# A two-layer hybrid transformer pair: the long convolutions' transforms as three products of high and low parts

## The reference

```python
def hyena_filter(n, w1, b1, freq, w2, b2, w3):
    ...                                  # a small MLP of the positions, two-sided, normalised to sum 1
    return two_sided / jnp.sum(jnp.abs(two_sided), axis=0, keepdims=True)
# per channel: g = cv * x1 (both short convolutions of projections of the normed input)
#              y = longconv(g, filter) + bias * g ; then y * x0, gated
```

## Time and profile before

| | |
|---|---|
| median of the runs | 1718.23 us (1717.48 to 1720.56) |
| the profiled execution | 1713.17 us |
| its span, first to last instruction | 1711.4 us |
| mean granted clock of TensorE | 0.98 |
| TensorE busy | 1606.1 us, 94% |
| VectorE, ScalarE, GpSimd busy | 63%, 49%, 9% |

### The profile page before, as it was taken

One profiled execution on the slowest core, in us unless ns is written; L12 is line 12 of the kernel. 1 busy time (PEld: TensorE's weight loads), 2 busy tenths in 40 slices (PEclk: granted clock), 3 DMA queues, 4 the chain that ended last, 5 costly groups with the idle time before them and its releaser, 6 DMA issues.

```text
span 1711.4 us, 23418 instructions
## 1 busy us (share of the span) xinstructions
PE 1606.1 (94%) x9108; PEld 1347.5 (79%) x9108; DVE 1077.7 (63%) x1999; ACT 830.6 (49%) x1511; POOL 147.2 (9%) x145
## 2 busy tenths in 40 slices
PE   7988999988889999989999998999997979999998
PEld 7967999877778888867778876887786868887886
DVE  7777777776667868754564657325546565464565
ACT  5855555555556555532203456533335255445564
POOL 0110111110000213100000010000001000000000
PEclk9989999999999999989999999999999989999999
DMA  7526655553265545434302111224422314242333
GB/s 251 168 88 212 225 189 186 173 197 101 98 193 173 181 134 173 144 109 165 136 1 74 50 50 37 87 86 172 136 74 87 111 49 131 79 136 76 122 111 123
DMA packets 61886, 217.69 MB, mean 127 GB/s; under 512 B 7888, under 2 KB 8144, under 8 KB 61648
## 3 DMA queue, kind: packets, MB, share of 16 engines
q1 hardware_dynamic: 58608, 212.40, 37.0%
q10 hardware_dynamic: 3168, 3.80, 0.7%
HBM read 215.09 MB, written 1.05 MB: 126 GB/s over the span
## 4 chain that ended last, share of the span: by engine, by line
PE 66%; DVE 12%; ACT 11%; issue 8%; POOL 2%; ACTq 1%; DMA 0%; DVEq 0%; POOLq 0%
PE PS L328 18%; PE PS L330 17%; PE PS L329 17%; DVE WL L304 3%; ACT WH L293 3%; PE PS L2642 2%; PE PS L2010 2%; PE PS L2019 2%; POOL AR L1532 2%; PE PS L779 1%; PE PS L2084 1%; PE PS L485 1%; PE PS L2061 1%; ACT TMP L396 1%; PE PS L2673 1%
## 5 line engine op out<-in xcount | busy, mean ns | idle before, releaser
L304 DVE TENSOR_TENSOR WL<-RAWB,WH 128x1024 fp32r<-128x1024 f32 x346 | 427.1, 1239 | 255.8 <-ACT WH L293 249.7
L328 PE MATMUL PS<-RH,WH 128*128 128x256 f32 (+1 forms) x1560 | 505.6, 324 | 19.7 <-DVE RH L509 4.0
L329 PE MATMUL PS<-RH,WH 128*128 128x256 f32 (+1 forms) x1560 | 492.6, 316 | 0.0
L330 PE MATMUL PS<-RH,WL 128*128 128x256 f32 (+1 forms) x1560 | 492.3, 316 | 0.0
L293 ACT CAST WH<-RAWB 128x1024 fp32r<-128x1024 f32 x346 | 358.5, 1041 | 247.6 <-PE PS L330 192.8
L328 PEld LDWEIGHTS PS<-RH,WH 128*128 128x128 f32 x1560 | 300.6, 193 | 55.1 <-issue 11.2
L328 PE MATMUL PS<-WH,RH 128*128 128x512 f32 (+1 forms) x768 | 307.2, 400 | 16.0 <-DVE WL L304 8.6
L329 PEld LDWEIGHTS PS<-RH,WH 128*128 128x128 f32 x1560 | 300.7, 193 | 18.2 <-issue 0.2
L330 PEld LDWEIGHTS PS<-RH,WL 128*128 128x128 f32 x1560 | 300.0, 192 | 18.5
L329 PE MATMUL PS<-WL,RH 128*128 128x512 f32 (+1 forms) x768 | 298.8, 389 | 0.0
L330 PE MATMUL PS<-WH,RH 128*128 128x512 f32 (+1 forms) x768 | 298.4, 389 | 0.0
(11 more groups left out here) (353 smaller groups left out, 1642.3 us busy)
## 6 DMA issues: line engine op xcount, KB each, us to landing
RAWB<-ws SPq DMA_DIRECT2D x394, 512.0 KB, 3.5
TMP<-gains ACTq DMA_DIRECT2D x8, 256.0 KB, 2.9
CS<-cs SPq DMA_DIRECT2D x1, 1472.0 KB, 9.1
X<-x SPq DMA_DIRECT2D x2, 512.0 KB, 4.0
X<-ctx SPq DMA_DIRECT2D x2, 512.0 KB, 8.1
AR<-dec ACTq DMA_DIRECT2D x2, 512.0 KB, 7.0
out<-X SPq DMA_DIRECT2D x4, 256.0 KB, 2.0
AR<-rgw SPq DMA_DIRECT2D x1, 512.0 KB, 5.1
```

The source lines that it names most:

```text
L304: dve.e.tensor_tensor(k.WL[:, i % SPL, :], k.RAWB[:, i % RAW, :], k.WH[:, i % SPL, :].bitcast(F32), ALU.subtract).then_inc(*dve.done("wl", i))
L328: pe.e.matmul(o, wh, xh, start=first, stop=False)
L329: pe.e.matmul(o, wh, xl, start=False, stop=False)
L330: return pe.e.matmul(o, wl, xh, start=False, stop=last)
```

## The change

The inputs and tables of both transforms become f32r pairs, high and low part, and each f32 matmul becomes three f32r ones (`three`): forward 24, inverse 48 in a unit.

- The forward table's pair lies in the WH/WL place of chunk last + 1 (`last` is the chunk of the last cv projection), written by ScalarE and VectorE at j = 7. The inverse table's pair lies in RH, written at j = 5.
- A turned input's pair lies in the places of chunks last and last - 1: ScalarE writes the high part from PSUM, VectorE the low part and frees the bank.
- Of the complex product's four results (SPC, C1) ScalarE writes the high part, GpSimd the low part, into a ring of six pairs in RH (unit 3's second half into the place of chunk last).
- The bias comes by a DMA on ScalarE's queue at j = 1 (a fifth row of `gains`), and GpSimd adds it to HF's real rows. L2321 goes; ScalarE copies the inverse's result from PSUM into G.
- The chunks last + 1 and last + 2 are split only when the places are free: ScalarE casts them after unit 3's high parts, VectorE after unit 3's product.

```diff
-        self.GT = k.ring("e2gt", [view(8192 + 1024 * i, 2, 512) for i in range(2)])
+        self.SPP = k.ring("e2spp", [(k.RH[:, a:a + 512], k.RH[:, a + 512:a + 1024]) for a in range(10240, 16384, 1024)])
+        self.last = k.ws.chunk("even2", "cv", 7)
+        self.HYB = view(9216, 1024)
...
-        self.dft = lambda n, f: k.C("dft")[:, 512 * n + 128 * f:512 * n + 128 * f + 128]
-        self.idft = lambda f: k.C("idft")[:, 256 * f:256 * f + 256]
+        self.idft = k.RH[:, 8192:9216], k.RH[:, 9216:10240]
+    def place(self, k, n):
+        return k.WH[:, n % SPL, :], k.WL[:, n % SPL, :]
+    def turned(self, k, u):
+        return [t.rearrange("p (a b) -> p a b", a=2) for t in self.place(k, self.last - u % 2)]
+    def forwards(self, k, n, f):
+        return [t[:, 512 * n + 128 * f:512 * n + 128 * f + 128] for t in self.place(k, self.last + 1)]
+    def back(self, f):
+        return [t[:, 256 * f:256 * f + 256] for t in self.idft]
+    def product(self, u, fb, part):
+        return self.C1 if (fb, part) == (1, 1) else self.SPC
+    def parts(self, k, u, fb, part):
+        if u == 3 and fb:
+            return [t[:, 512 * part:512 * part + 512] for t in self.place(k, self.last)]
+        return self.SPP.of(u, fb, part)
...
-SPEC_STEPS = [(*SPEC_UNITS[u], p) for u, p in rounds([3] * 4)]
+SPEC_PARTS = [(0, 0), (0, 1), (1, 0), (1, 1)]
+SPEC_STEPS = rounds([3] * 4)
...
@@ even2_pe
-    for q, c, p in SPEC_STEPS:
+    for u, p in SPEC_STEPS:
+        q, c = SPEC_UNITS[u]
         if p == 0:
             for tb in range(2):
                 b = k.ps.take(pe, s, "gt", q, c, tb)
                     t = pe.e.transpose(b[:, 128 * jj:128 * jj + 128], L.G[:, 4 * c + jj, c0:c0 + 128], k.ident)
                 t.then_inc(*pe.done(s, "gt", q, c, tb))
         elif p == 1:
+            pe.wait_ge(*k.DVE.at(s, "table", 0))
             for tb in range(2):
-                pe.wait_ge(*k.ACT.at(s, "gt", q, c, tb))
-            g = L.GT.of(s, q, c)
+                pe.wait_ge(*k.DVE.at(s, "gt", q, c, tb))
+            gh, gl = L.turned(k, u)
             for fb in range(2):
                 for part in range(2):
-                    b = k.ps.take(pe, s, "u", q, c, fb, part)
+                    b = k.ps.take(pe, s, "u", u, fb, part)
                     for n in range(2):
-                        mm = pe.e.matmul(b, L.dft(n, 2 * part + fb), g[:, n, :], start=n == 0, stop=n == 1)
-                    mm.then_inc(*pe.done(s, "u", q, c, fb, part))
-            L.GT.free(pe, s, q, c)
+                        mm = three(pe, b, L.forwards(k, n, 2 * part + fb), (gh[:, n, :], gl[:, n, :]), n == 0, n == 1)
+                    mm.then_inc(*pe.done(s, "u", u, fb, part))
         else:
-            rows = [L.SPC.of(s, q, c, 0, 0), L.SPC.of(s, q, c, 1, 0), L.SPC.of(s, q, c, 0, 1), L.C1.of(s, q, c, 1, 1)]
-            pe.wait_ge(*k.DVE.at(s, "spec", q, c))
+            pe.wait_ge(*k.DVE.at(s, "table", 1))
+            for fb, part in SPEC_PARTS:
+                pe.wait_ge(*k.POOL.at(s, "low", u, fb, part))
+            rows = [L.parts(k, u, f % 2, f // 2) for f in range(4)]
             for jj in range(4):
                 b = k.ps.take(pe, s, "y", q, 4 * c + jj)
+                cols = slice(128 * jj, 128 * jj + 128)
                 for f in range(4):
-                    mm = pe.e.matmul(b[:, 0:256], rows[f][:, 128 * jj:128 * jj + 128], L.idft(f), start=f == 0, stop=f == 3)
+                    mm = three(pe, b[:, 0:256], [t[:, cols] for t in rows[f]], L.back(f), f == 0, f == 3)
                 mm.then_inc(*pe.done(s, "y", q, 4 * c + jj))
-            for name in ((0, 0), (1, 0), (0, 1)):
-                L.SPC.free(pe, s, q, c, *name)
-            L.C1.free(pe, s, q, c, 1, 1)
+            for fb, part in SPEC_PARTS:
+                L.SPP.free(pe, u, fb, part)
...
@@ even2_act
     for j in range(8):
-        cast_to(k, act, k.ws.chunk(s, "x1", j) + 2)
+        cast_to(k, act, min(k.ws.chunk(s, "x1", j) + 2, L.last))
         x = k.sq.take(act, s, "x1", j)
         conv3_act(k, act, s, "x1", j, x, k.P("ecw", 24 + 8 + j), k.P("ecb", 8 + j))
-        cast_to(k, act, k.ws.chunk(s, "cv", j) + 2)
+        cast_to(k, act, min(k.ws.chunk(s, "cv", j) + 2, L.last))
         conv3_act(k, act, s, "cv", j, L.G[:, j, :], k.P("ecw", 24 + 16 + j), k.P("ecb", 16 + j))
-    for q, c, p in SPEC_STEPS:
+        if j == 1:
+            act.wait_ge(*k.DVE.at(s, "hf", 1, 3))
+            act.wait_ge(*k.PE.at(s, "hf", 1, 3))
+            act.e.dma_start(L.HYB, k.gains[4]).then_inc(k.s_hyb, 16)
+        if j == 5:
+            act.wait_ge(k.s_cs2, 16)
+            act_(L.idft[0], k.C("idft"), ACT.Copy).then_inc(*act.done(s, "table", 1))
+        if j == 7:
+            act.wait_ge(*k.PE.at("weights", before(k, L.last + 1)))
+            act_(L.place(k, L.last + 1)[0], k.C("dft"), ACT.Copy).then_inc(*act.done(s, "table", 0))
+    for u, p in SPEC_STEPS:
+        q, c = SPEC_UNITS[u]
         if p == 0:
-            g = L.GT.take(act, s, q, c)
+            act.wait_ge(*k.PE.at("weights", L.last - u % 2))
+            act.wait_ge(*k.PE.at(s, "u", u - 2, 1, 1))
             for tb in range(2):
                 act.wait_ge(*k.PE.at(s, "gt", q, c, tb))
-                act_(g[:, tb, :], k.ps.of(s, "gt", q, c, tb), ACT.Copy).then_inc(*act.done(s, "gt", q, c, tb))
-                k.ps.free(act, s, "gt", q, c, tb)
+                act_(L.turned(k, u)[0][:, tb, :], k.ps.of(s, "gt", q, c, tb), ACT.Copy).then_inc(
+                    *act.done(s, "gt", q, c, tb))
+        elif p == 1:
+            for fb, part in SPEC_PARTS:
+                if u == 3 and fb:
+                    act.wait_ge(*k.PE.at(s, "u", 2, 1, 1))
+                else:
+                    L.SPP.take(act, u, fb, part)
+                act.wait_ge(*k.DVE.at(s, "spec", u, fb, part))
+                act_(L.parts(k, u, fb, part)[0], L.product(u, fb, part).of(u, fb, part), ACT.Copy).then_inc(
+                    *act.done(s, "high", u, fb, part))
+            if u == 3:
+                act.wait_ge(*k.PE.at(s, "u", 3, 1, 1))
+                cast_to(k, act, L.last + 2)
+        else:
+            for j in range(4 * c, 4 * c + 4):
+                act.wait_ge(*k.PE.at(s, "y", q, j))
+                act_(L.G[:, j, 256 * q:256 * q + 256], k.ps.of(s, "y", q, j)[:, 0:256], ACT.Copy).then_inc(
+                    *act.done(s, "conv", j))
+                k.ps.free(act, s, "y", q, j)
...
@@ even2_dve
     for j in range(8):
-        rest_to(k, dve, k.ws.chunk(s, "x1", j) + 2)
+        rest_to(k, dve, min(k.ws.chunk(s, "x1", j) + 2, L.last))
...
-        rest_to(k, dve, k.ws.chunk(s, "cv", j) + 2)
+        rest_to(k, dve, min(k.ws.chunk(s, "cv", j) + 2, L.last))
         conv3_dve(k, dve, s, "cv", j, L.G[:, j, :], k.P("ecw", 16 + j), k.P("ecw", 48 + 16 + j))
...
-    for q, c, p in SPEC_STEPS:
-        if p == 1:
+        if j == 5:
+            dve.wait_ge(*k.ACT.at(s, "table", 1))
+            v.tensor_tensor(L.idft[1], k.C("idft"), L.idft[0].bitcast(F32), ALU.subtract).then_inc(*dve.done(s, "table", 1))
+        if j == 7:
+            hi, lo = L.place(k, L.last + 1)
+            dve.wait_ge(*k.ACT.at(s, "table", 0))
+            v.tensor_tensor(lo, k.C("dft"), hi.bitcast(F32), ALU.subtract).then_inc(*dve.done(s, "table", 0))
+    for u, p in SPEC_STEPS:
+        q, c = SPEC_UNITS[u]
+        if p == 0:
+            gh, gl = L.turned(k, u)
+            for tb in range(2):
+                dve.wait_ge(*k.ACT.at(s, "gt", q, c, tb))
+                v.tensor_tensor(gl[:, tb, :], k.ps.of(s, "gt", q, c, tb), gh[:, tb, :].bitcast(F32), ALU.subtract).then_inc(
+                    *dve.done(s, "gt", q, c, tb))
+                k.ps.free(dve, s, "gt", q, c, tb)
+        elif p == 1:
             cc = slice(512 * c, 512 * c + 512)
+            dve.wait_ge(*k.POOL.at(s, "biased"))
             for fb in range(2):
...
-                v.tensor_tensor(a, a, y, ALU.subtract).then_inc(*dve.done())
+                v.tensor_tensor(a, a, y, ALU.subtract).then_inc(*dve.done(s, "spec", u, fb, 0))
...
-                v.tensor_tensor(x, x, y, ALU.add).then_inc(*dve.done(s, "spec", q, c))
-        elif p == 2:
-            for j in range(4 * c, 4 * c + 4):
-                g = L.G[:, j, 256 * q:256 * q + 256]
-                dve.wait_ge(*k.PE.at(s, "y", q, j))
-                v.scalar_tensor_tensor(g, g, k.P("hyb", j), k.ps.of(s, "y", q, j)[:, 0:256], ALU.mult,
-                                       ALU.add).then_inc(*dve.done(s, "conv", j))
-                k.ps.free(dve, s, "y", q, j)
+                v.tensor_tensor(x, x, y, ALU.add).then_inc(*dve.done(s, "spec", u, fb, 1))
+    rest_to(k, dve, L.last + 2)
...
@@ even2_dve, stage x0
+        dve.wait_ge(*k.ACT.at(s, "conv", j))
...
@@ even2_pool
     L, s = Even2(k), "even2"
+    pool.wait_ge(k.s_hyb, 16)
+    for f in range(2):
+        hr = L.HF[:, f, :]
+        pool.wait_ge(*k.DVE.at(s, "hf", 1, f))
```

(54 more changed lines are left out.)

## The result

Over 20 runs each the changed kernel took 1722.03 us in the median and the one before 1714.76; the ratio is 1.0039, with a 95% interval of 1.0028 to 1.0050: 6.7 us slower by the ratio (4.8 to 8.6), 7.3 by the two medians. The profiled execution of the changed kernel has a span of 1715.0 us in 1716.77. That is only 3.6 us more than the profiled execution before: it reached the stretch of the change 1.1 us earlier and took 2.6 us less behind it, in stages that the edit hardly touches.

What follows compares the result with a forecast made beforehand. TensorE bounded the stretch before; the chain was expected to move to VectorE: 4.0 us less, then 7.3 for the port and 3.2 for the clock, 6.5 us more, 1724.7 us on the median; range 1715 to 1730.

Steps and rivals of the forecast that it cites:

- TensorE's own work: Four forward and four inverse units: three products of parts replace each f32 product, 10.3 us less if TensorE stayed busy.
- The opening: Start of the stretch: the table's and first unit's low parts on VectorE delay TensorE's first forward by 3.6 us.
- The hand-offs between units: VectorE waits for ScalarE and low parts: 2.65 us between units 0 and 1, 4.15 between 1 and 2.
- The port: VectorE operations reading two SBUF tensors wait while GpSimd subtracts: 13 times 0.56 us, 7.3 us on the chain.
- meetings: Spectrum operations with two SBUF inputs arriving while GpSimd works: three per unit, one between units 2 and 3, 13 in all.
- The tail: After the last spectrum: one high part, one GpSimd low part and three hand-offs, 2.3 us, before the last inverse.
- The clock: TensorE's granted clock falls after idle times at the opening and ahead of the last inverse: 1.6 us each, 3.2.
- A third fall: An idle time of 2 to 3 us ahead of the first inverse slows only what has slack; nothing counted.
- Rival 1: GpSimd's and VectorE's operations don't meet: 4.0 us less, 1.5 back for the clock, 1715.7 us; chance 0.15.
- Rival 2: GpSimd and VectorE meet but the clock stays at 1.00: 3.3 us more, 1721.5 us; chance 0.15.
- Rival 3: TensorE stays the bound in the stretch: 10.3 us less, 1707.9 us; chance 0.05 together with another rival.

Runs made afterwards that it cites:

- e7: The inverse half of the change alone, forwards in f32 as in the kernel before: stretch 57.47 us, ratio to before 0.9987.
- e6: The forward half of the change alone, inverse in f32 as in the kernel before, nothing on GpSimd: stretch 58.47 us, ratio to before 0.9988.
- e5: Changed kernel with spectrum products in place in PSUM, forward table split earlier, units 0 and 1 turned ahead of the last projection: stretch 52.27 us, ratio to before 0.9965.
- e1: Changed kernel with the spectrum's products left in place in PSUM, so no operation reads two SBUF tensors: stretch 56.98 us, ratio to before 0.9981.
- e2: Changed kernel with each GpSimd subtraction covering 8 of 512 columns: stretch 56.48 us, ratio to before 0.9979.
- e4: Changed kernel with useless TensorE products ahead of the first forward (15) and the last inverse (18): stretch 62.03 us, ratio to before 1.0020.
- e8: The inverse half of the change alone, with the spectrum's products in place in PSUM: stretch 54.98 us, ratio to before 0.9957.

## Why the prediction was right

The forecast was 6.5 us more on the kernel; 6.7 was measured, and 7.3 in the stretch. The forecast of 1724.7 us stood on a median of three runs, 1718.23; over 20 runs the kernel before has 1714.76, and the changed one 1722.03 in place of 1724.7. That 6.7 comes so near to 6.5 is partly luck, as its interval is 4.8 to 8.6 and the terms below are off in both directions. The steps of the sum are better evidence. They are these, with the stretch starting at 842.67 before and 841.59 after:

- **TensorE's own work.** 5.83 us for an inverse at full clock (e7, 892.69 to 898.52) and 5.55 for a forward (e6, 855.58 to 861.13), predicted 5.76 and 5.44. That it is worth nothing while VectorE leads is the changed kernel; that 6.6 us come of it once both repairs are in is e5.
- **The opening.** The first forward starts at 847.34 in place of 844.77 in a stretch that begins 1.1 us earlier: 3.65 us late, predicted 3.6. Without its waits the first unit of VectorE would begin at 851.26 (0.61 ahead of its second operation), 9.7 after the start; the sum with its clock term said 9.7.
- **The hand-offs between units** were 2.5 and 3.6 us (861.00 to 863.46, 873.34 to 876.90, counted from where a next operation would have followed), predicted 2.65 and 4.15. The second is shorter because ScalarE's four copies out of PSUM take 1.1 us up to the next operation where 1.5 had been counted.
- **The port.** 13 meetings predicted, 13 in the trace. Half a unit takes 5.18 us (886.67 to 891.85) where it was 3.98, so 0.60 each in place of 0.56, 7.8 us in place of 7.3. e1 and e2 show that it is these operations and GpSimd's time. One reading behind the step can't be followed in the earlier trace rows: L1479 starts at 557.39, when the GpSimd operation shown there has ended. The trace does show a GpSimd operation beside it, this one:

```profile
556.34 1.72 POOL L1532 TENSOR_TENSOR AR<-AR 128x256 f32<-128x256 f32 x1
```

- **The tail.** The last spectrum ends at 897.10 and the last inverse starts at 899.37: 2.3 us as predicted, after 4.35 idle (4.4).
- **The clock.** 1.5 us at the opening, predicted 1.6 (the first forward takes 7.06 us, 847.34 to 854.40, where 5.55 is its time at full clock). In the last inverse the term was too small: that took 8.37 us where 5.8 is its time at full clock, 2.6 lost in place of 1.6, since the clock stayed low nearly to its end. This is the one term off by more than 0.6 us, and with the port's 0.5 more and the hand-offs' 0.8 less it makes the 0.8 between 65.3 and 66.15. A third fall, after the first inverse's start, has slack, as predicted, but uses all of it up: ScalarE's third high part of unit 1 waits for that inverse to free its place until 870.85, where VectorE's result was there at 870.65, and the sum behind it takes 1.40 us in place of 1.24.

```profile
870.85 0.63 ACT L2209 ACTIVATE RH<-AR 128x512 fp32r<-128x512 f32 x1 [2.13 <-PE PS L330]
```

Rival 1 (no meetings) is what e1 and e2 build: their stretches are 1.9 and 2.4 us under before's, and the rival's sum said 2.5. Rival 2 (the clock stays) is what e4 builds, by keeping TensorE busy: 3.2 measured, 3.3 said. Rival 3 would have needed both repairs, and even e5 doesn't reach it. What the prediction had not seen: each half of the change alone is no slower than before, 0.4 and 1.4 us faster by the stretch (the intervals of the ratios end at 1.0000 and 0.9998), and both together are 7.3 slower. The f32 forwards cover the meetings (e7), and without the meetings VectorE keeps up with the short forwards (e6); together they take time from TensorE and give it to VectorE in the same units, until VectorE leads.

## What to carry to other kernels

Before one engine's work is cut by giving high and low parts to others, lay the new chain out engine by engine for one unit: here VectorE had 18 us of slack beside TensorE's 58.6, and a late opening, low parts, hand-offs and meetings used it up. Where GpSimd is to work beside VectorE, leave one input of VectorE's operations in PSUM: it costs no instruction, and was worth 9 us of 66 where VectorE led (the clock ahead of the last inverse included), and 2.5 of 57 where TensorE led. Time the halves of a change alone; two that lose nothing can lose together.

## What the runs showed of the hardware

- A VectorE operation that reads two tensors in SBUF and a GpSimd one that does so too hardly overlap in these traces, whichever comes first. The longest of VectorE's is in e7: it starts at 865.12, 0.11 us behind GpSimd's (865.01 to 866.29), takes 1.71 us and ends 0.54 behind it. The 0.74 us of GpSimd in e2 are the other direction.
- Products written back in place to PSUM cost VectorE nothing: 0.69 us from PSUM and SBUF into PSUM (L2391 in e1), as into SBUF.
- The same idle time of 3.84 us at the opening was followed by different stretches of low clock. The changed kernel and e1, the latter from the first forward on:

```profile
852.46:858.76 6.30, 6.30 (x15) 4.95 (x16) 2.54 (x5) 0.00 (x0) 0.00 (x0) 0.52 0.00 0
```

  3.36 us at 0.53 in the one, 6.30 at 0.52 in the other: 1.6 and 3.0 us lost, worked out from these rows (length times the missing part of the clock). What decides the length stays open.
- An idle time of 2.44 us ahead of the first inverse was followed by a fall in the changed kernel (0.63 over the next 4.66 us), while in e4 the same 2.44 us left the clock at 1.00 over the next 4.67 us. The idle time alone didn't decide it there; what did stays open.
- Why e8 gained 7.4 us by the runs and 3.9 in the stretch isn't settled; single executions of these kernels reach the stretch up to 6 us apart (840.91 in e8, 846.71 in e1), with other clocks in stages that the edits don't touch (0.97 in e8 from 720 to 780 us, 0.89 in e1, 0.91 in the kernel before).
